# A two-layer-type transformer block on one core: dilated attention in pairs of heads, fuller loads of short slabs, and other places for the linear-attention jobs

## The reference, cut to what matters

```python
h = rmsnorm(x, norm_mix_g);  proj = h @ w_in
q_a, k_a, v_a, q_b, k_b, v_b, gl_a, gl_b = split(proj)
o_a = dilated_attention(q_a, k_a, v_a)      # 3 groups (window, dilation) of 4 heads, head size 64
o_b = stick_breaking_attention(q_b, k_b, v_b)
merged = sigmoid(gl_a + b) * (o_a @ w_up_dil) + sigmoid(gl_b + b) * (o_b @ w_up_sb)
x = x + merged @ w_out
x = x + square(relu(rmsnorm(x) @ w_mlp_in)) @ w_mlp_out
...
# second block, per chunk of 64 tokens:
o = scores @ v + (q * exp(b)) @ S;  S = exp(b_end) * S + (k * exp(b_end - b)).T @ v
o = rmsnorm(o, gla_norm) * silu(r)
m = sigmoid(ga) * y_pool + sigmoid(gb) * (o @ w_gla_out);  h = h + m @ w_out
```

## Time and profile before

| | us |
|---|---|
| median of 3 runs | 1498.28 (1496.57 to 1498.34) |
| profiled execution, own time | 1497.24 |
| its span, first to last instruction | 1495.5 |
| TensorE matmuls busy | 1470.0 (98%) |
| VectorE busy | 807.9 (54%) |
| ScalarE busy | 496.6 (33%) |
| GpSimd busy | 87.6 (6%) |
| DMA | 129.81 MB, mean 87 GB/s |
| granted TensorE clock | 0.996 of full speed |

### The profile page before, as it was taken

How to read it: one execution, slowest core, us unless ns; L and a number is a source line. 1 busy time by engine, 2 the same in 40 slices (tenths; PEclk the granted TensorE clock), 3 DMA queues, 4 the chain that set the end, 5 groups by cost and what they waited for, 6 DMA issues and landing times.

```text
span 1495.5 us, 19062 instructions
## 1 busy us (share of the span) xinstructions
PE 1470.0 (98%) x7860; PEld 1183.8 (79%) x7860; DVE 807.9 (54%) x1022; ACT 496.6 (33%) x671; POOL 87.6 (6%) x108
## 2 busy tenths in 40 slices
PE   7999999999999999999999999999999999999997
PEld 6887788777888888888878987777788888888886
DVE  7544543565766344453558867548756445354442
ACT  4123332553433122221243344324443222132233
POOL 6000000000020000000031200000020000000001
PEclk9999999999999999999999999999999999999998
DMA  5222112202322322323223212221232232332321
GB/s 172 85 85 85 52 63 85 85 8 64 125 87 85 113 84 96 100 84 108 90 85 99 75 46 72 85 81 60 99 107 90 90 107 84 98 98 84 113 85 56
DMA packets 127430, 129.81 MB, mean 87 GB/s; under 512 B 2314, under 2 KB 126836, under 8 KB 127364
## 3 DMA queue, kind: packets, MB, share of 16 engines
q1 hardware_dynamic: 127364, 128.86, 26.7%
HBM read 126.75 MB, written 2.10 MB: 86 GB/s over the span
## 4 chain that ended last, share of the span: by engine, by line
PE 92%; DVE 5%; ACT 2%; issue 1%; DMA 0%; ACTq 0%; SPq 0%; DVEq 0%
PE ps L1598 81%; PE ps L1594 3%; DVE wl L993 1%; PE ps L1935 1%; DVE SQ L1513 1%; PE ps L1842 1%; PE ps L1828 1%; PE ps L1815 1%; PE ps L1723 1%; PE ps L1728 0%; DVE wl L1064 0%; ACT wh L635 0%; PE ps L1759 0%; PE ps L1753 0%; PE ps L1703 0%
## 5 line engine op out<-in xcount | busy, mean ns | idle before, releaser
L1598 PE MATMUL ps<-Ah,wh 128*128 128x512 f32 x1008 | 402.3, 399 | 1.7 <-DVE wl L993 1.4
L1598 PE MATMUL ps<-Al,wh 128*128 128x512 f32 x1008 | 398.6, 395 | 0.0
L1598 PE MATMUL ps<-Ah,wl 128*128 128x512 f32 x1008 | 396.7, 394 | 0.0
L1598 PE MATMUL ps<-Bh,wh 128*128 128x512 f32 x800 | 318.1, 398 | 5.4 <-DVE wl L993 4.2
L1598 PE MATMUL ps<-Bl,wh 128*128 128x512 f32 x800 | 316.4, 395 | 0.0
L1598 PE MATMUL ps<-Bh,wl 128*128 128x512 f32 x800 | 314.6, 393 | 0.0
L1064 DVE TENSOR_TENSOR wl<-raw,wh 128x1024 fp32r<-128x1024 f32 x124 | 156.0, 1258 | 139.4 <-ACT wh L686 138.9
L1598 PEld LDWEIGHTS ps<-Ah,wh 128*128 128x128 f32 x1008 | 189.5, 188 | 50.2 <-DVE wl L993 2.6
L686 ACT ACTIVATE wh<-raw 128x1024 fp32r<-128x1024 f32 x124 | 131.2, 1058 | 290.3 <-PE ps L1598 290.3
L1598 PEld LDWEIGHTS ps<-Ah,wl 128*128 128x128 f32 x1008 | 189.7, 188 | 43.3
L1598 PEld LDWEIGHTS ps<-Al,wh 128*128 128x128 f32 x1008 | 189.4, 188 | 42.0 <-issue 0.2
(11 more groups left out here) (243 smaller groups left out, 1179.3 us busy)
## 6 DMA issues: line engine op xcount, KB each, us to landing
raw<-in_w_in SPq DMA_DIRECT2D x39, 1024.0 KB, 5.6
raw<-in_w_ff SPq DMA_DIRECT2D x32, 1024.0 KB, 5.1
raw<-in_w_mlp_in SPq DMA_DIRECT2D x16, 1024.0 KB, 5.4
raw<-in_w_mlp_out SPq DMA_DIRECT2D x16, 1024.0 KB, 4.8
raw<-in_w_out SPq DMA_DIRECT2D x8, 1024.0 KB, 4.8
arena<-in_x SPq DMA_DIRECT2D x4, 512.0 KB, 6.7
raw<-in_w_up_sb SPq DMA_DIRECT2D x4, 512.0 KB, 3.5
raw<-in_w_pool_out SPq DMA_DIRECT2D x4, 512.0 KB, 3.4
```

What stands on the lines that cost most here:

```text
L1598: last = pe.matmul(dense_psum(t_ps, kind), a[:, k, :], b[:, o0 + k, col0:col0 + S1], start=start, stop=stop)
```

## The change

Four edits, with the same arithmetic:

1. **Dilated units are pairs of heads.** There are 8 units instead of 16, each with both heads of a pair: head b uses rows 64b to 64b+63 of the array and PSUM bank 2+b, and the heads' matmuls on the dilated groups alternate. A step has one whole slab, so 12 steps take the place of 21. The logits have two buffers of two heads; `PT` and the banks of the transposes have one buffer of two heads. In a step TensorE now does slab, `oa_turn`, `dil_pv`, `dil_turn`, `dil_scores`; ScalarE copies the transposes of unit u-3 in step u, in which TensorE also uses them, after `oa_hi_copy` where there is one. VectorE's additions, maxima and normalisations take both heads at once where they can.
2. **Loads of short slabs fill a buffer**: one load of 8 slabs for `w_up_dil`, two of 4 slabs for `w_up_sb`, two of 4 for `w_gla_out_2`.
3. **The sigmoid table** is loaded before ScalarE's last two V copies instead of after them.
4. **Linear attention**: the second `kv` job goes from after T2_GY+12 to after T2_GY+10, the output jobs start one slab earlier with heads' pairs four slabs apart instead of three, and the two `o_norm` of a pair are two slabs apart instead of one.

```diff
-DIL_STEPS = 21
+DIL_STEPS = 12
...
     def wide(name, base, tiles, kt=KT):
-        for i in range(0, tiles, 2):
-            add(name, base + i * P, kt, 2)
+        n = 2 * KT // kt
+        for i in range(0, tiles, n):
+            add(name, base + i * P, kt, n)
...
     between[T2_GY + 8] += [("kv", 0)]
-    between[T2_GY + 12] += [("kv", 1)]
-    t = T2_GY + 14
+    between[T2_GY + 10] += [("kv", 1)]
+    t = T2_GY + 13
     for j in range(2):
-        at = t + 3 * j
+        at = t + 4 * j
         between[at] += [("o_mm", j, 0)]
         between[at + 1] += [("o_mm", j, 1)]
         between[at + 2] += [("o_stat", 2 * j), ("o_stat", 2 * j + 1)]
         between[at + 3] += [("o_norm", 2 * j)]
-        between[at + 4] += [("o_norm", 2 * j + 1)]
-    assert t + 7 < T2_GO
+        between[at + 5] += [("o_norm", 2 * j + 1)]
+    assert t + 9 < T2_GO
...
-        Lg = region(11008, 2, 512)
+        Lg = [region(11008, 2, 512), region(12032, 2, 512)]
...
-            n, j = 3 - u // 4, u % 4
+            n, jp = 3 - u // 2, u % 2
...
                 act.wait_ge(pt_psum, u + 1)
-                if u >= 2:
-                    act.wait_ge(pv_done, u - 1)
-                act.activation(PT[:, u % 2, 0:c1 + 2 * P], ps[:, 4 + u % 2, 0:c1 + 2 * P], ACT.Copy)\
-                   .then_inc(pt_copied, 1)
+                if u >= 1:
+                    act.wait_ge(pv_done, u)
+                act.activation(PT[:, :, 0:c1 + 2 * P], ps[:, 4:6, 0:c1 + 2 * P], ACT.Copy).then_inc(pt_copied, 1)
...
             for u in range(DIL_STEPS):
-                if u >= 16:
-                    convert(T_QKV_B + u - 16 + 1)
-                elif u % 2 == 0:
-                    convert(T_GATE_A + u // 2 + 1)
-                if u >= 8 and u % 4 == 0:
-                    oa_hi_copy(u // 4 - 2)
-                if 0 <= u - 2 < 16:
-                    dil_copy(u - 2)
-                if 0 <= u - 1 < 16:
+                convert(T_GATE_A + u + 1)
+                if u >= 5 and u % 2 == 1:
+                    oa_hi_copy((u - 5) // 2)
+                if 0 <= u - 3 < 8:
+                    dil_copy(u - 3)
+                if 0 <= u - 1 < 8:
                     dil_exp(u - 1)
-                if u % 2 == 0 and 2 <= u <= 16:
-                    s = u // 2
-                    gate(T_GATE_A + s - 1, GA[:, s - 1, :], s - 1)
-
-
-            for t in range(T_QKV_B + DIL_STEPS - 16, T_GATE_B):
+                if 1 <= u <= 8:
+                    gate(T_GATE_A + u - 1, GA[:, u - 1, :], u - 1)
+
+
+            for t in range(T_GATE_A + DIL_STEPS, T_GATE_B):
                 convert(t + 1)
                 i = t - T_QKV_B - 8 - 2
                 if i >= 0:
                     v_copy(6 + i, Vnb[:, :, i * P:(i + 1) * P])
+            act.preload_act_table(ACT.Sigmoid)
...
             for u in range(DIL_STEPS):
-                if 0 <= u - 4 < 16:
+                if 0 <= u - 4 < 8:
                     dil_norm(u - 4)
-                if u > 16:
-                    qkv_b(T_QKV_B + u - 17)
-                elif u % 2 == 0 and u >= 2:
-                    scaled(T_GATE_A + u // 2 - 1, GA[:, u // 2 - 1, :], ONE)
-                if u >= 16:
-                    convert(T_QKV_B + u - 16 + 1)
-                elif u % 2 == 0:
-                    convert(T_GATE_A + u // 2 + 1)
-                if u >= 8 and u % 4 == 0:
-                    oa_lo(u // 4 - 2)
-                if 0 <= u - 1 < 16:
+                if u > 8:
+                    qkv_b(T_QKV_B + u - 9)
+                elif u >= 1:
+                    scaled(T_GATE_A + u - 1, GA[:, u - 1, :], ONE)
+                if 0 <= u - 1 < 8:
                     dil_softmax(u - 1)
-
-
-            for t in range(T_QKV_B + DIL_STEPS - 16, T_GATE_B + 1):
+                convert(T_GATE_A + u + 1)
+                if u >= 5 and u % 2 == 1:
+                    oa_lo((u - 5) // 2)
+
+
+            for t in range(T_GATE_A + DIL_STEPS, T_GATE_B + 1):
...
             def dil_scores(u):
-                n, j, nb, w, c1 = dil_unit(u)
-                b = DH * (j % 2)
-                if u >= 2:
-                    pe.wait_ge(logits_done, 2 * (u - 1))
-                pe.matmul(ps[:, 2 + u % 2, 0:c1], qa[b:b + DH, j // 2, n * P:(n + 1) * P],
-                          ka[b:b + DH, j // 2, (n + 1 - nb) * P:(n + 1) * P], start=True, stop=True)
+                n, jp, nb, w, c1 = dil_unit(u)
+                if u >= 1:
+                    pe.wait_ge(logits_done, 3 * u)
+                for b in range(2):
+                    rows = slice(DH * b, DH * b + DH)
+                    pe.matmul(ps[:, 2 + b, 0:c1], qa[rows, jp, n * P:(n + 1) * P],
+                              ka[rows, jp, (n + 1 - nb) * P:(n + 1) * P], start=True, stop=True)
                 for g in (1, 2):
-                    i, col = 2 * g + j // 2, c1 + (g - 1) * w
+                    i, col = 2 * g + jp, c1 + (g - 1) * w
                     for c in range(4):
-                        mm = pe.matmul(ps[32 * c:32 * c + 32, 2 + u % 2, col:col + w],
-                                       qa[b:b + DH, i, n * P + 32 * c:n * P + 32 * c + 32],
-                                       ka[b:b + DH, i, c * P:c * P + w], start=True, stop=True)
+                        for b in range(2):
+                            rows = slice(DH * b, DH * b + DH)
+                            mm = pe.matmul(ps[32 * c:32 * c + 32, 2 + b, col:col + w],
+                                           qa[rows, i, n * P + 32 * c:n * P + 32 * c + 32],
+                                           ka[rows, i, c * P:c * P + w], start=True, stop=True)
                 mm.then_inc(scores_done, 1)
 
...
             pe.wait_ge(late_scaled, 2)
             for u in range(DIL_STEPS):
-                if u < 16:
-                    t = T_GATE_A + u // 2
-                    if u % 2 == 0:
-                        slab_start(t)
-                    mm = products(t, t % 2, KT, Ah, Al, 0, ONE, 4 * (u % 2), 4 * (u % 2) + 4)
-                    if u % 2:
-                        mm.then_inc(slab_done, 1)
-                    if u == 0:
-                        pe.wait_ge(evac_done, T_GATE_A)
-                        v_turn(5, vt[:, 1, :])
-                else:
-                    full_slab(T_QKV_B + u - 16, Ah, Al, 0, ONE)
-                if u >= 8 and u % 4 == 0:
-                    oa_turn(u // 4 - 2)
-                if 0 <= u - 2 < 16:
+                full_slab(T_GATE_A + u, Ah, Al, 0, ONE)
+                if u == 0:
+                    pe.wait_ge(evac_done, T_GATE_A)
+                    v_turn(5, vt[:, 1, :])
+                if u >= 5 and u % 2 == 1:
+                    oa_turn((u - 5) // 2)
+                if 0 <= u - 3 < 8:
+                    dil_pv(u - 3)
+                if 0 <= u - 2 < 8:
                     dil_turn(u - 2)
-                if 0 <= u - 3 < 16:
-                    dil_pv(u - 3)
-                if u < 16:
+                if u < 8:
                     dil_scores(u)
 
 
-            for t in range(T_QKV_B + DIL_STEPS - 16, T_GATE_B):
+            for t in range(T_GATE_A + DIL_STEPS, T_GATE_B):
```

More of the change, by code:

```diff
@@ new lines, in dil_softmax @@
+                dve.tensor_tensor(lg[:, :, c1:ncol].rearrange("p b (g x) -> p b g x", g=2),
+                                  ps[:, 2:4, c1:ncol].rearrange("p b (g x) -> p b g x", g=2),
+                                  D12[:, 2 * jp:2 * jp + 2, :, P - w:P], ALU.add).then_inc(logits_done, 1)
+                dve.wait_ge(logits_done, 3 * u + 3)
+                two = slice(2 * u, 2 * u + 2)
+                dve.tensor_reduce(stat[:, 0, two], lg[:, :, 0:ncol], AX_X, ALU.max).then_inc(max_done, 1)
@@ L1208, in dil_norm @@
+                two = slice(2 * u, 2 * u + 2)
+                dve.wait_ge(probs_ready, 2 * u + 2)
+                dve.reciprocal(stat[:, 3, two], stat[:, 2, two]).then_inc(rden_done, 1)
                 dve.wait_ge(rden_done, u + 1)
                 dve.wait_ge(pv_done, u + 1)
-                if j == 0 and k >= 2:
+                if jp == 0 and k >= 2:
                     dve.wait_ge(oT_psum, k - 1)
-                dve.tensor_scalar(onat[k % 2][:, j * DH:(j + 1) * DH], ps[:, 7, j * DH:(j + 1) * DH],
-                                  stat[:, 3, u:u + 1], None, ALU.mult).then_inc(o_norm, 1)
+                cols = slice(2 * jp * DH, (2 * jp + 2) * DH)
@@ L1215, in oa_lo @@
+                dve.tensor_tensor(onat[k % 2][:, cols].rearrange("p (b x) -> p b x", b=2),
+                                  ps[:, 7, cols].rearrange("p (b x) -> p b x", b=2),
+                                  stat[:, 3, two].unsqueeze(2).to_broadcast([P, 2, DH]), ALU.mult).then_inc(o_norm, 1)
             def oa_lo(k):
@@ L1731, in dil_scores @@
                 mm.then_inc(scores_done, 1)
             def dil_turn(u):
-                n, j, nb, w, c1 = dil_unit(u)
-                pe.wait_ge(probs_ready, u + 1)
-                if u >= 2:
-                    pe.wait_ge(pt_copied, u - 1)
-                for i in range(nb):
```

(42 more changed lines are left out.)

41 lines of the change are left out of this document (18 added, 23 removed).

## The result

The changed kernel takes 1500.19 us (median of 17 runs, 1497.91 to 1502.67), the kernel before 1497.31 us beside it (17 runs). The ratio is 1.0017, with a 95% interval of 1.0009 to 1.0024: 2.9 us slower by the medians (1.3 to 3.6 by the interval), a small loss but not none, and above the range of the prediction. The profiled run of the changed kernel, at 1497.91 us, is its fastest; its span is 1496.2 us.

A forecast was written before the change was run, and what follows sets the result against it. TensorE, busy nearly throughout, was taken as the bound; dilated attention -0.45, sigmoid table -0.8, loads -1.2 and linear attention +0.2 summed to -2.25 us, a median of 1496.0 us. The range was 1492.5 to 1498.8 us.

The forecast's parts named there:

- New wait 2: Behind oa_turn in steps 5, 7 and 9, TensorE waits for the copy to PT: 1.7 + 1.7 + 1.5 = 4.9 us.
- New wait 1: Ahead of slab 19, converted only behind the last V copy, TensorE waits 1.85 us.
- `kv`: Linear attention: behind the moved second kv job, TensorE waits 2.1 us ahead of slab T2_GY+12.
- New neighbours: Dilated attention: products and transposes beside different work, 0 to 0.8 us, taken as 0; transposes ahead of scores lose 0.5.
- Scores on the dilated groups: L1731 in pairs takes 0.57, 0.52, 0.52, 0.52 us, twice each: 4.3 us instead of 6.6, 2.3 saved.
- rival A: Small matmuls gain more, L1731 at one head's price, and oa_turn waits are shorter: 2.4 us more, 1493.6 us; chance 0.22.
- Rival B: Row halves of L1731 don't overlap in the dilated scores: 2.3 us lost, 1497.7 us; chance 0.12.
- the window group: Dilated attention: L1724 for two heads costs one head's price, 0.63 and 0.42 us a pair, 4.6 us saved.
- the loads: First slab of w_up_sb: its load starts a group of slabs earlier, so TensorE's wait goes, 1.2 us saved.
- the `o_norm` waits: Linear attention: two slabs apart, the second o_norm wait (2.07 us) goes and the first (0.42) stays.
- C: Dilated attention: ScalarE is late for PT in all steps, five other products wait too, 5.4 us, 1501.4 us; chance 0.06.
- D: Neither the wait at oa_turn nor at slab 19 arises: 6.8 us more saved, 1489.2 us; chance 0.06.

The follow-up runs named there:

- e5_no_waits: Changed kernel with PT copied ahead of oT, slab 19 converted ahead of the last V copy, second kv back at T2_GY+12: 1485.74 us (before 1497.46).
- e10_pairs_alone: Kernel before with head pairs alone, PT copied ahead of oT and slab 19 converted ahead of the last V copy: 1490.33 us (before 1496.75).
- b1: Kernel before with TensorE made to wait behind oa_turn of steps 8, 12 and 16 until oT is taken: 1503.49 us (before 1496.8).
- e1_copy_first: Changed kernel with ScalarE's copy to PT ahead of the copy of oT in steps 5, 7 and 9: 1491.09 us (before 1496.8).
- e2_fill: Changed kernel with 7 unused matmuls between oa_turn and the products of steps 5, 7 and 9: 1496.67 us (before 1496.8).
- e9: Kernel before with three TensorE waits added ahead of plain slabs 5, 8 and 11 of the first projections: 1508.63 us (before 1496.75).
- e11_one_start: e5_no_waits with transposes ahead of products, both heads' products grouped by tile shape, one start flag for both heads: 1483.07 us (before 1497.55).
- e6_order: e5_no_waits with transposes ahead of products and both heads' products grouped by tile shape, each head keeping its start flag: 1483.13 us (before 1497.46).

## Why the prediction was wrong

**The step that failed** is "New wait 2" with its neighbours "New wait 1" and `kv`: each wait was found where it was put and nearly in its length (1.73 for 1.85; 1.56, 1.56 and 1.35 for 1.7, 1.7 and 1.5; 1.96 for 2.1), but it was priced at its length alone. The sum has no term for the clock. By e5_no_waits 8.16 us of waits cost 14.6, 6.4 more. The profile of the kernel before gave no warning, since its wait of 2.07 us is followed by full clock. One profile shows one case: in e10_pairs_alone half clock follows the same wait (1041.36 to 1043.42):

```profile
1043.00:1045.00 2.00, 1.57 (x4) 1.28 (x5) 1.57 (x3) 1.05 (x2) 0.00 (x0) 0.67 0.21 52
1045.00:1047.00 2.00, 2.00 (x6) 1.51 (x6) 0.00 (x0) 0.00 (x0) 0.00 (x0) 0.50 0.62 210
```

Over the 16 profiles, in stretches of half a microsecond behind each wait and without the start and the last stage, 16 of 32 waits of 1.35 to 2.56 us are followed by lower clock, with 1.7 us lost (in b1 3.4). So a wait of this size cost about 0.9 us more on average. In the dilated attention the three at `oa_turn` cost 8.6 - 4.5 = 4.1 us of clock by e1_copy_first and 3.0 by e2_fill, 1.0 to 1.4 us each. Whether that stage is dearer isn't shown: in the profiles half clock followed 7 of 12 waits behind `oa_turn` and 9 of the 20 others.

**New neighbours**, taken at 0 and with 0.5 us for the transposes ahead of scores, cost 1.5. Most of it is in two places: the second L1761 of a pair takes 0.59 us instead of 0.48 six times and 0.37 instead of 0.27 twice, and L1744 and L1747 take 0.50 + 0.53 instead of 0.44 + 0.44 in the five steps in which products stand ahead of them and scores behind. In all, from start to start, products went from 12.6 to 13.4 us and transposes from 6.6 to 7.3 (before and e5_no_waits). The upper ends (0.8 + 0.5) were too low as well.

**Scores on the dilated groups** are cheaper than forecast: a pair takes 0.60, 0.49, 0.39 and 0.28 us as w falls, nearly what one head took the earlier trace rows, 3.6 us in all for 4.3. This is a piece of rival A. The issue bound of 16 ns didn't hold; 32 instructions in 0.28 us are 9 ns each. Rival B is refuted, and so, for tiles of 64 x 32 at full clock, is the floor of 25 ns of the Trainium skill, page "TensorE: Matmul & The Clock Gate", section "Back-to-back issue gap".

**Right** were the window group (0.63 and 0.42 us a pair), the sigmoid table, the loads (1.2 us to 0.2), the `o_norm` waits, and the rivals C and D as losers: no product but those behind `oa_turn` waited.

Together: waits -0.7, L1731 -0.7, neighbours +1.0, the load's wait +0.2 for the 0.2 us that stay, the small terms of the linear attention -0.2, clock +6.4 less some 0.9 that the kernel before loses to its own wait of 2.07 us (an estimate from the average above), in sum +5.1 us. The forecast was 2.3 us below before; corrected it is 2.8 above, where 2.9 was measured. That it meets to a tenth is chance: the clock's part comes from e5_no_waits and carries some 2 us to either side, and by the clocks on record it is 10.4 - 5.6 = 4.8 us and not 5.5.

Open is what decides whether a wait is followed by half clock. In like positions it was and was not, between profiles of the same code. Neither the length alone (0.88 us with, 2.56 without) nor the small work beside it (e9) does.

## What to carry to other kernels

Price an idle wait of TensorE at more than its length where the engine is otherwise always busy: here it was 1.6 to 2.0 times by the medians of six kernels, 1.8 in the one with the most waits in it (e5_no_waits, 14.6 us for 8.16). Where a merged step puts two kinds of work into one queue (the copy to `PT` behind the copy of `oT`), order them by who waits; this one swap was worth 8.6 us, no less than the pairs themselves (6.4 in e10_pairs_alone). A wait that can't be removed can be worth filling, even with useless matmuls: 3.0 us for three waits here. An order without the waits is worth more. And where a profile is of the fastest run, look at the clocks of the others before taking it for the kernel.

## What was not expected of the hardware

Eight tiles of 64 x 32 on both row halves run at the time of four: 32 matmuls of 32 columns in 0.28 us. Matmuls of one tile shape behind each other are cheaper than the same ones mixed: with both heads' products grouped (e11_one_start, step 7), 8 of L1763 took 0.93 us, in two groups of 4 (e5_no_waits, step 7) they took 0.49 + 0.59; 32 of the small tiles took 0.58 us, in two groups 0.71. And a second `start` in a bank, on other columns, while a sum there was unfinished, gave a wrong output without an error (e6_order against e11_one_start).
